# Two chained transformer blocks on one core: residual kept with features on partitions, sums of squares added on GpSimd

## The reference

```python
def first_block(x, mem, ...):
    h = x
    proj = rmsnorm(h, norm_mix_g) @ w_in             # q, k, v, u, y
    attn = dilated_mixture_attention(rope(q), rope(k), v)
    rec = bidirectional_rglru(conv(u), ...) * gelu(y)
    h = h + concat([attn, rec]) @ w_out
    h = h + memory_cross_attention(rmsnorm(h, norm_cross_g), rmsnorm(mem, norm_mem_g), w_cq, w_ck, w_cv, w_co)
    hid = square(relu(rmsnorm(h, norm_mlp_g) @ w_mlp_in))          # 4096 wide
    h = h + hid @ w_mlp_out
    return rmsnorm(h, norm_final_g)

def second_block(x, ...):
    for l in range(2):
        z = rmsnorm(x, ln_mix[l]) @ w_in[l]          # four mixers' inputs and four gates
        merged = sum(sigmoid(gate[n]) * (mixer[n](z) @ w_branch[l, n]) for n in range(4))
        x = x + merged @ w_out[l]
        g, u = split(rmsnorm(x, ln_ffn[l]) @ w_gate_up[l])         # 2816 each
        x = x + (silu(g) * u) @ w_down[l]
    return x
```

## Time and profile before

| | |
|---|---|
| time, median of 3 runs | 1211.79 us (1210.22 to 1213.87) |
| profiled execution: its time | 1213.07 us |
| profiled execution: its span | 1211.1 us, so 1.97 lie outside the span |
| mean granted clock of TensorE in it | 0.999 of full speed |
| TensorE busy | 1198.2 us, 10044 matmuls |
| VectorE, ScalarE, GpSimd busy | 842.4, 689.9 and 40.0 us |
| weights and other DMA | 211.5 MB, 175 GB/s in the mean |

### The profile page before, as it was taken

One profiled execution on the slowest core, in us unless ns is written; L12 is line 12 of the kernel. 1 busy time (PEld: TensorE's weight loads), 2 busy tenths in 40 slices (PEclk: granted clock), 3 DMA queues, 4 the chain that ended last, 5 costly groups with the idle time before them and its releaser, 6 DMA issues.

```text
span 1211.1 us, 23685 instructions
## 1 busy us (share of the span) xinstructions
PE 1198.2 (99%) x10044; PEld 1121.4 (93%) x10044; DVE 842.4 (70%) x1195; ACT 689.9 (57%) x1144; POOL 40.0 (3%) x88
## 2 busy tenths in 40 slices
PE   8999999999999999999999999999999999999998
PEld 8998989998899999899999998899999989999987
DVE  6997767654476878988656554658789877666544
ACT  5897655553366764792544543557665925544432
POOL 1200100000000000011000000000000100000000
PEclk9999999999999999999999999999999999999999
DMA  9643445565544435434565565535344426555552
GB/s 366 233 147 128 173 146 192 192 207 180 205 165 149 142 138 174 143 139 159 190 199 185 189 198 204 174 140 174 108 172 146 169 106 209 175 191 192 183 203 102
DMA packets 30617, 211.50 MB, mean 175 GB/s; under 512 B 3376, under 2 KB 3760, under 8 KB 5680
## 3 DMA queue, kind: packets, MB, share of 16 engines
q1 hardware_dynamic: 30224, 209.84, 49.8%
q10 hardware_dynamic: 288, 0.14, 0.0%
HBM read 208.92 MB, written 1.05 MB: 173 GB/s over the span
## 4 chain that ended last, share of the span: by engine, by line
PE 85%; ACT 6%; DVE 5%; issue 2%; DMA 1%; SPq 0%; DVEq 0%; ACTq 0%
PE bank L552 84%; ACT w_hi L1226 3%; DVE w_lo L1750 2%; ACT W L1542 2%; PE bank L671 1%; DMA ring<-weight_pieces 1%; PE bank L919 1%; DVE x_lo L1869 0%; DVE stat L2205 0%; ACT W L1226 0%; DVE W L2145 0%; DVE W L2278 0%; ACT W L1513 0%; ACT W L1508 0%; ACT W L1498 0%
## 5 line engine op out<-in xcount | busy, mean ns | idle before, releaser
L1750 DVE TENSOR_TENSOR w_lo<-ring,w_hi 128x2048 fp32r<-128x2048 f32 (+1 forms) x180 | 409.1, 2273 | 238.0 <-ACT w_hi L1226 237.3
L1226 ACT ACTIVATE w_hi<-ring 128x1024 fp32r<-128x1024 f32 (+1 forms) x368 | 366.5, 1047 | 232.7 <-PE bank L552 210.5
L552 PE MATMUL bank<-x_hi,w_hi 128*128 128x256 f32 x1840 | 260.5, 281 | 1.5 <-issue 1.4
L552 PE MATMUL bank<-x_hi,w_lo 128*128 128x256 f32 x1840 | 252.8, 277 | 3.1 <-DVE w_lo L1750 3.1
L552 PE MATMUL bank<-x_lo,w_hi 128*128 128x256 f32 x1840 | 247.5, 277 | 0.2 <-DVE x_lo L1869 0.2
L552 PEld LDWEIGHTS bank<-x_hi,w_hi 128*128 128x128 f32 x1840 | 230.5, 188 | 6.0 <-ACT x_hi L1226 1.9
L552 PEld LDWEIGHTS bank<-x_hi,w_lo 128*128 128x128 f32 x1840 | 229.0, 188 | 4.3 <-DVE w_lo L1750 4.1
L552 PEld LDWEIGHTS bank<-x_lo,w_hi 128*128 128x128 f32 x1840 | 226.8, 188 | 0.6 <-DVE x_lo L1869 0.6
L552 PE MATMUL bank<-W 128*32 128x32 f32 (+8 forms) x1552 | 75.6, 244 | 3.8 <-issue 2.2
L552 PE MATMUL bank<-w_hi,hid_hi 128*128 128x512 f32 x304 | 76.6, 389 | 0.0
L552 PE MATMUL bank<-w_lo,hid_hi 128*128 128x512 f32 x304 | 76.6, 389 | 0.0
(11 more groups left out here) (269 smaller groups left out, 1208.9 us busy)
## 6 DMA issues: line engine op xcount, KB each, us to landing
ring<-weight_pieces SPq DMA_DIRECT2D x191, 1024.0 KB, 4.9
W<-x_features SPq DMA_DIRECT2D x4, 256.0 KB, 4.9
ring<-weight_pieces SPq DMA_DIRECT2D x2, 512.0 KB, 5.7
h<-x SPq DMA_DIRECT2D x2, 512.0 KB, 6.7
W<-rg_weights SPq DMA_DIRECT2D x1, 1024.0 KB, 11.2
xs<-mem_features SPq DMA_DIRECT2D x1, 1024.0 KB, 12.8
oT<-mem SPq DMA_DIRECT2D x1, 1024.0 KB, 14.2
row<-rows SPq DMA_DIRECT2D x1, 1024.0 KB, 8.2
```

Source lines behind the costliest of these rows:

```text
L552: return nc.tensor.matmul(out, lhsT, rhs, start=first, stop=last)
L1226: return nc.scalar.activation(out, in_, ACT.Copy, scale=scale)
L1750: v.tensor_tensor(whole(w_lo, q), rows, whole(w_hi, q).bitcast(F32), ALU.subtract).then_inc(s_weight_low, 1)
```

## The change

The residual h keeps features on partitions, `[P, KT, S]`, from wout of the first block to the output.

- wout, co, down and wd become feature form; `token_weights` goes. down and wd have eight accumulators of 256 columns in place of four of 512, so 24 products of 512 columns a piece become 48 of 256, whose weights alternate between the two halves of the piece. Their drains become eight plain additions of 128x256.
- The transposes of h at six norms go. ScalarE copies `x_hi` (at ln_mix) or `y_hi` (at the others) straight from h, two feature tiles after each drain (`norm_part`), VectorE subtracts (`x_low`). y_hi and y_lo share memory with `xs` and `oT`.
- ScalarE squares 128x512 of h into one of four places (`square`), GpSimd adds these (`add_squares`: three additions of 128x512, one of 128x256). TensorE sums over partitions with a column of ones (new steps `columns`, and `layerstat`, which moves behind a[1]), and VectorE starts rsqrt from that bank.
- For `ln_mix_0` VectorE adds squares weighted with the gain (`add_weighted`, eight linked operations), the fourth square of ScalarE waits for the second pair of them; `rstd_row` transposes four columns in place of two; the final scale (`finalscale`) moves from ScalarE to VectorE, eight operations.
- In up, the row of 1/rms squared is made between the halves of up.1 and applied to every product by VectorE; ScalarE's Relu goes. In gu, VectorE has one more multiplication with the row.
- The first GEMM behind a norm (cq, a, up, gu; wout of the layers as before) interleaves its two halves over the feature tiles, in two banks.
- In the SBUF all moved operands (x, y, hid) lie ahead of the weights. Rope tables have memory of their own. The output is written as `[P, KT*S]` and turned on the host.

```diff
-FEATURE = ("u", "y", "q", "k", "ck", "cq", "a", "f", "e", "up", "gu", "gate")
+FEATURE = ("u", "y", "q", "k", "ck", "cq", "a", "f", "e", "up", "gu", "gate", "wout", "co", "down", "wd")
...
-        sb("between_operands", [P, 44])
+        xs = sb("xs", [P, TT, D])
+        oT = sb("oT", [P, KT, S])
+        y_hi = nc.alloc_sbuf_tensor_at("y_hi", [P, KT, S], F32R, offset=nc.sbuf_base - 4 * 2 * KT * S)
+        y_lo = nc.alloc_sbuf_tensor_at("y_lo", [P, KT, S], F32R, offset=nc.sbuf_base - 4 * KT * S)
+        W = sb("W", [P, ARENA])
+        arena0 = nc.sbuf_base - 4 * ARENA
+        junk = sb("junk", [P, D], BF16)
+        sb("between_operands", [P, 40])
         ring = sb("ring", [P, RING, PIECE])
...
-        h = sb("h", [P, TT, D])
...
+        h = sb("h", [P, KT, S])
...
-        steps += [*ups[:4], ("params",), *ups[4:]]
+        steps += [pe(ups[0]), act(ups[0]), ("columns", "norm_mlp_g"), ("low", ups[2][-1]), dve(ups[0]), *ups[1:4], ("params",), *ups[4:]]
...
-            steps += [a[0], ("high", f0[-1]), ("low", f0[-1]), ("layerstat", l), a[1], f0, ("finalscale", l)]
+            steps += [a[0], ("high", f0[-1]), ("low", f0[-1]), a[1], ("layerstat", l), f0, ("finalscale", l)]
...
-                        turns(f"{name}.{j}", lambda k, tt: h[:, tt, (2 * j + k) * P:(2 * j + k + 1) * P], 2)
+                elif kind in ("columns", "layerstat"):
+                    name = step[1] if kind == "columns" else ("final", "ln_mix_1")[step[1]]
...
+                    pe.wait_ge(s_stat_sum, feature_stats.index(name) + 1)
+                    if name == "final":
+                        pe.wait_ge(s_weighted, 4)
+                    bank = fill(f"{name}.sum", "g" if name in ("norm_mlp_g", "ln_ffn_0", "ln_ffn_1") else "m")
+                    for n, src in enumerate((square_sum[:, 0, :], rrow) if name == "final" else (square_sum[:, 0, :],)):
+                        for tt in range(TT):
+                            ins = mm(bank[:, TT * n + tt:TT * n + tt + 1], src[:, tt * P:(tt + 1) * P], ones_col, True, True)
...
-                                ins = mm(acc[tt, c][:, :], x[:, 2 * j + k, tt * P:(tt + 1) * P], w[:, k, 512 * c:512 * c + 512],
+                                ins = mm(acc[m][:, 0:S], half_of(w, q, k)[:, m * P:(m + 1) * P], x[:, 2 * j + k, :],
                                          i == j == k == 0, i == 2 and k == 1 and j == count - 1)
...
+            def add_squares(stat):
+                n = feature_stats.index(stat)
+                for i in range(1, 4):
+                    pool.wait_ge(s_square, 4 * n + i + 1)
+                    if stat == "final":
+                        pool.wait_ge(s_weighted, i)
+                    nc.gpsimd.tensor_tensor(square_sum[:], square_sum[:], square_place(i), ALU.add).then_inc(s_square_added, 1)
+                    pool.wait_ge(s_square_added, 3 * n + i)
+                nc.gpsimd.tensor_tensor(square_sum[:, 0, :], square_sum[:, 0, :], square_sum[:, 1, :], ALU.add).then_inc(s_stat_sum, 1)
...
+            def norm_part(name, i):
+                x = x_hi if name[:6] == "ln_mix" else y_hi
...
+                for job in producers(name, i):
+                    wait_drained(act, job)
+                for k in (2 * i, 2 * i + 1):
+                    ins = copy(x[:, k, :], h[:, k, :], gain[:, k:k + 1])
+                ins.then_inc(s_norm_all, 1)
+
+            def square(name, i):
+                n = feature_stats.index(stat_of(name))
+                if i == 0 and n:
+                    wait_filled(act, f"{feature_stats[n - 1]}.sum")
+                elif i == 3:
+                    act.wait_ge(s_square_added, 3 * n + 1)
+                    if feature_stats[n] == "final":
+                        act.wait_ge(s_weighted, 2)
+                nc.scalar.activation(square_place(i), h[:, 2 * i:2 * i + 2, :], ACT.Square).then_inc(s_square, 1)
...
+            def x_low(name, i):
...
+                    ins = v.scalar_tensor_tensor(lo[:, k, :], h[:, k, :], gain[:, k:k + 1], hi[:, k, :].bitcast(F32), ALU.mult, ALU.subtract)
...
+            def add_weighted(i):
+                dve.wait_ge(s_square, 4 * feature_stats.index("final") + i + 1)
...
+                    ins = v.scalar_tensor_tensor(rrow[:], src[:, k % 2, :], weight[:, k:k + 1], rrow[:], ALU.mult, ALU.add)
...
-                                drains(v.scalar_tensor_tensor(hh, wait_filled(dve, job)[:], rs[:, tt:tt + 1], hh, ALU.mult, ALU.add), job)
+                                drains(v.tensor_tensor(h[:, m, :], wait_filled(dve, job)[:, 0:S], h[:, m, :], ALU.add), job)
...
-                        dve.wait_ge(s_relu, m + 1)
-                        drains(v.tensor_tensor(product[:, m % 2, :], wait_filled(dve, job)[:], product[:, m % 2, :], ALU.mult), job)
...
+                        link(v.scalar_tensor_tensor(hidden, bank, 0.0, scaled, ALU.max, ALU.mult))
+                        drains(v.tensor_tensor(hidden, bank, hidden, ALU.mult), job)
```

498 lines of the change are left out of this document (268 added, 230 removed).

## The result

| | before | changed |
|---|---|---|
| median of 20 runs each | 1210.69 us (1209.63 to 1214.36) | 1214.51 us (1210.32 to 1218.13) |
| ratio of the medians, 95% interval | | 1.0022 (1.0012 to 1.0033) |
| mean granted clock, over the runs | 0.998 to 1.0 (runs taken beside the experiments) | 0.994 to 0.999 |

What follows compares the result with a forecast made beforehand. TensorE, busy 1198.2 of 1211.1 us, was taken as the bound, losing 2.54 to 2.97 at norms. Terms summed to 9.9 gained, less 2 for collisions, about 8, so 1204 for the median; range 1196 to 1214, held at some 0.8.

Steps and rivals of the forecast that it cites:

- wout to cross, and the memory's products: Norm before cross attention: 2.54 us of stall gone less 0.25 for sum products, 2.3; memory's products gain at most 0.3.
- co to MLP: Norm before up: stall gone, but TensorE waits 1.3 us in up.1 for the row of 1/rms squared; net +0.9.
- pace of down and wd: Their 1824 products of 256 columns run at up's pace of 113.4 ns, so the new form costs 0.
- ln_mix_0: First norm of the layers, with two statistics: weighted adds delay f0's weights, f0 ends late; loss 1 to 2.4, taken 2.0.
- wout to FFN, wout's pace, two layers: FFN norms gain 2.25 us each, 4.5; the layers' wout goes from 118 to 113.4 ns a product, 1.8.
- wd to ln_mix_1: Norm between layer 0's wd and layer 1: loss falls from 2.97 to 1.15 us, a gain of 1.8.
- collisions: GpSimd's last additions held by VectorE's low-weight splits at about two norms: 2 us lost in all.
- The dearest rival: down and wd run at kr's pace of 120 ns a product: 12.0 us more, 1216; chance 0.14.
- a linked hand-over each about 0.45: At ln_mix_0, each of VectorE's eight weighted adds takes about 0.45 us including its linked hand-over.
- the second rival: GpSimd's last adds collide at every norm and TensorE waits at the sum product: 1209; chance 0.12.
- written bank by bank in piece 0, so this wait I cost at nothing: Start of down: its eight accumulators need banks up and gu just left, filled one by one; wait costed at nothing.
- the norms give all: Rival: no collision (+2), first norm of the layers keeps level (+2), VectorE in time in up.1 (+1.3): 1199; chance 0.15.

Runs made afterwards that it cites:

- e2: Changed kernel with 28 unused products of 256 columns ahead of TensorE's wait for the sum products of ln_mix_0; 1208.34 us, ratio 0.9963.
- e4: Changed kernel with GpSimd's additions at all six norms cut to one column, the sums otherwise left out; 1206.70 us, ratio 0.9961.
- e6: Changed kernel with the products of the low weights last in the first piece of down and wd; 1211.40 us, ratio 0.9999.
- e12: Changed kernel with 28 unused 256-column products ahead of ln_mix_0's wait, low weights last in down's and wd's first piece, up's row behind up.1; 1204.44 us.
- e16: Changed kernel with only its start edited, 34 small and 6 wide unused products for 8 wide, so 64 more lie ahead; 1207.03 us, ratio 0.9968.
- e15: Changed kernel with ln_mix order mended, low weights last in down and wd, up's row behind up.1, and 64 more unused products at its start; 1200.38 us.
- e3: Changed kernel with ln_mix_0's eight weighted adds cut to one one-column operation per pair, the weighted sum left out; 1209.78 us, ratio 0.9978.
- e1: Changed kernel with a place of its own for each square of ln_mix_0, so ScalarE and GpSimd don't wait for the weighted adds; 1211.38 us, ratio 0.9994.
- e14: Changed kernel with ln_mix order mended, low weights last, up's row behind up.1, and 64 unused 32-column products ahead of ln_mix_0's sums; 1212.89 us.

## Why the prediction was wrong

The sum had a gain of 7.9; the profiled spans show a loss of 1.6, and the ratio of the medians one of 2.7. Gains in us, by the stages of the first profile of before; collisions were a term of their own in the sum and lie inside the measured rows.

| term | forecast | measured | |
|---|---|---|---|
| wout to cross, and the memory's products | +2.6 | +2.3 | held (1.9 to 3.3 by other profiles) |
| co to MLP | +0.9 | -1.2 | y waits, beside the adds |
| pace of down and wd | 0 | 0 | held: 113.3 |
| ln_mix_0 | -2.0 | -5.7 | wait, then clock |
| wout to FFN, wout's pace, two layers | +6.3 | +5.5 | nearly |
| starts of gu and wd, two layers | 0 | -2.5 | low weights late: 2.1; 0.4 not followed |
| wd to ln_mix_1 | +1.8 | +1.0 | x_lo beside the adds (8 in 5.35) |
| pace of layer 1's wd | 0 | -0.5 | not followed |
| tail | +0.3 | +0.4 | held |
| collisions | -2 | (above) | |
| mixers | 0 | -2.9 | stops, and 1.7 for the late piece; against before again (-0.9 against the first) |

**Right.** The transposes were worth what the rows said where nothing collided: 2.3 at the first norm, and 2.7 to 2.8 in each layer for norm and wout together (3.15 forecast; wout's pace came to 114.7 and not 113.4). The dearest rival fell: down's 16 products take 1.81, that is 113 ns, against the 226.9 for two in the earlier trace rows.

```profile
299.04 1.98 PE L551 MATMUL bank<-hid_hi,w_lo 128*128 128x256 f32 x16
300.85 1.98 PE L551 MATMUL bank<-hid_hi,w_hi 128*128 128x256 f32 x16
```

The wait for the row in up.1 came at its forecast length, 1.3, in part by luck: the row began at T + 11.6 and not T + 9.65 and TensorE was there at T + 10.3 and not T + 8.4, both some 1.9 late. w_hi of f0 came at T + 14 as forecast (it ended at T + 14.1).

**Wrong: ln_mix_0's term.** The step "a linked hand-over each about 0.45" failed: beside GpSimd a weighted add takes 0.95 to 1.02, so the chain of eight takes 6.8 us (351.76 to 358.58) and not 3.6. The consequence was also read at the wrong place: I asked when f0's weights would be ready and not when the sums would. GpSimd's sum was ready at T + 14.8, behind w_hi, f0 began at T + 16.5, and it ended at T + 24.5 and not at 20 to 21.3. And I put no price on an idle TensorE beyond the idle time itself; e2 shows that the fall of the clock behind it was about as dear as the wait. This term is the largest single miss, 3.7 of the 9.5 us between the sum and the spans.

**Wrong: collisions in one direction.** The earlier trace rows show GpSimd held by VectorE, and I costed only that, at the sum products. e4 shows the other direction: without the additions six y_lo take 2.46 and not 4.41, and the weighted adds 0.50 and not 0.95. No single wait at the sums (the second rival's mechanism) appeared but at ln_mix_0; the price was paid one step earlier, at the norms' low parts.

**Wrong: "written bank by bank in piece 0, so this wait I cost at nothing".** The banks were indeed free. What was late was the low half of the weights, which that very order asks for ahead of the first product; e6 took both waits away by order alone.

**Not thought of: the mixers.** By the change 408 more products lie ahead of layer 0's burst in TensorE's program and 648 ahead of layer 1's. That the place decides over the stops is shown by e12 to e16: products that change nothing else, added at two different places, shorten or remove them. That the stop is the wait for code itself is argued, from "issue" and from the instruction packets being the only DMA then; it was not tried apart. e16's 6.5 us are more than the two stops (3.2) in the profile of the changed kernel. The clock behind stops has a part in the rest: the mean granted clock is 0.9963 over the changed kernel's runs and 0.9981 over e16's, worth 2.1 us by an estimate from these two (their difference times 1210). What is left, about 1 us, stays open.

The rival "the norms give all" had 1199, and with the waits mended, but for those at the norms' low parts, e15 gives 1200.4. That it comes so near is in part luck: e15 has also lost the stop in layer 1 that before has, and before was never shifted. Outside the mixers e15's span is 8.0 to 8.3 us shorter than the two profiles of before, about the gain of 8 that was forecast; the other 2.3 to 4.3 lie in the mixers, and a shift alone might give them to before as well, which was not tried. Between the changed kernel and e15 lie nearly 13 us by the ratios: waits, the clock and stops, which another order and 64 unused products took away.

## What to carry to other kernels

Where work moves to GpSimd at a point where VectorE is on the path, cost the collision from both sides, and hold GpSimd back until VectorE's short operations are done. Price a stall of TensorE by what comes behind it too: here 3.16 us of waiting cost 2.6 more in slow products. Ask whether useful or useless wide products can fill it. When a small edit moves time in a stage that it does not touch, look for stops marked "issue" and shift the program by some harmless instructions, the kernel before as well as the changed one, before believing in the edit.

## What the runs showed of the hardware

- The granted clock fell to 0.50 behind an idle stretch of 3.16 us with eight products of one column, in e3 behind 0.95 with the same eight (0.58 over 3 us), and once in the kernel before behind a stop of 2.2; behind the changed kernel's stops of 1.56 and 1.69 it stayed at 1.0. It fell also among 64 products of 32 columns (0.11 us each at the full clock), without any idle time (0.71 and 0.61 over 20 us); with 28 products of 256 columns in the wait it stayed at 1.0.
- A GpSimd addition of 128x512 took 1.28 to 2.08 us in the changed kernel, and 3.75 beside a w_lo (3.77 in e1); VectorE's operations of 128x256 with two inputs went from 0.41 to 0.73 (y_lo) and from 0.50 to 0.95 (weighted adds) beside it.
- TensorE stopped 1.3 to 2.4 us from start to start inside 192 products of 32 columns, at the same product in both profiles of before, and at the same count of products in the changed kernel and its variants; 64 more products ahead removed the stops (e14, e15, e16), 28 shortened them (0.6 to 1.6).
